# Expert routing weights by indirect DMA into device memory, inputs before outputs

## The reference

```python
s1 = jnp.einsum('thd,nd->thn', q[..., :PEER_HALF], subkeys1)
s2 = jnp.einsum('thd,nd->thn', q[..., PEER_HALF:], subkeys2)
v1, i1 = lax.top_k(s1, 16); v2, i2 = lax.top_k(s2, 16)
cand = v1[..., :, None] + v2[..., None, :]
vals, pos = lax.top_k(cand, 16)
ids = i1[pos // 16] * 128 + i2[pos % 16]
g = softmax(vals)
a = jnp.einsum('td,thkd->thk', xt, u_tab[ids])
hid = gelu(a) * g
y = jnp.einsum('thk,thkd->td', hid, v_tab[ids])
```

## Time and profile before

| | |
|---|---|
| median of three executions | 1153.8 us (1153.69 to 1155.7) |
| span of the profiled execution | 1152.6 us |
| instructions | 21629 |
| PE busy | 1102.2 us |
| DVE busy | 914.7 us |
| ACT busy | 479.6 us |
| POOL busy | 15.2 us |
| moved by DMA | 177.62 MB |

### The profile page before, as it was taken

One profiled execution on the slowest core, in us unless ns is written; L12 is line 12 of the kernel. 1 busy time (PEld: TensorE's weight loads), 2 busy tenths in 40 slices (PEclk: granted clock), 3 DMA queues, 4 the chain that ended last, 5 costly groups with the idle time before them and its releaser, 6 DMA issues.

```text
span 1152.6 us, 21629 instructions
## 1 busy us (share of the span) xinstructions
PE 1102.2 (96%) x7340; PEld 1004.3 (87%) x7340; DVE 914.7 (79%) x1706; ACT 479.6 (42%) x718; POOL 15.2 (1%) x20
## 2 busy tenths in 40 slices
PE   7779999799999999999998999999999999999996
PEld 7657898799999999999997888888888888888885
DVE  3246547668889998899898767777799999999997
ACT  4145444344445444434333444444344444444332
POOL 0310000000000000000000000000000000000000
PEclk9889999999999999999999999999999999999998
DMA  7664245432444434232223555555566656665563
GB/s 245 168 203 146 94 166 179 128 129 92 141 134 146 129 127 130 96 103 92 91 91 116 183 193 196 188 198 190 174 182 181 174 178 176 179 177 178 178 180 110
DMA packets 88102, 177.62 MB, mean 154 GB/s; under 512 B 16384, under 2 KB 44288, under 8 KB 88064
## 3 DMA queue, kind: packets, MB, share of 16 engines
q1 hardware_dynamic: 88064, 177.11, 48.1%
HBM read 176.03 MB, written 1.05 MB: 154 GB/s over the span
## 4 chain that ended last, share of the span: by engine, by line
PE 81%; DVE 7%; DMA 5%; SPq 2%; ACT 2%; issue 2%; DVEq 0%; ACTq 0%
PE ps L1328 29%; PE ps L1255 28%; PE ps L1222 12%; PE ps L1166 5%; PE ps L1307 4%; DMA w_raw<-in_w_in_dram 4%; SPq L260 1%; DVE w_lo L817 1%; DMA v_raw<-in_peer_v_dram 1%; DVE uT_raw L986 1%; PE ps L1120 1%; ACT w_hi L508 1%; PE ps L1159 1%; DVE v_lo L969 1%; ACT v_hi L602 1%
## 5 line engine op out<-in xcount | busy, mean ns | idle before, releaser
L1255 PE MATMUL ps<-act_hi,uT_hi 128*128 128x256 f32 x1024 | 295.3, 288 | 0.0
L1255 PE MATMUL ps<-act_hi,uT_lo 128*128 128x256 f32 x1024 | 289.8, 283 | 0.0
L1255 PE MATMUL ps<-act_lo,uT_hi 128*128 128x256 f32 x1024 | 289.6, 283 | 0.0
L1255 PEld LDWEIGHTS ps<-act_hi,uT_hi 128*128 128x128 f32 x1024 | 196.3, 192 | 2.1
L1255 PEld LDWEIGHTS ps<-act_lo,uT_hi 128*128 128x128 f32 x1024 | 196.2, 192 | 2.1
L1255 PEld LDWEIGHTS ps<-act_hi,uT_lo 128*128 128x128 f32 x1024 | 195.9, 191 | 0.0
L1328 PE MATMUL ps<-v_hi,hid_hi 128*128 128x512 f32 x512 | 164.8, 403 | 5.0 <-DVE v_lo L969 4.1
L1328 PE MATMUL ps<-v_hi,hid_lo 128*128 128x512 f32 x512 | 159.0, 392 | 0.0
L1328 PE MATMUL ps<-v_lo,hid_hi 128*128 128x512 f32 x512 | 158.7, 391 | 0.0
L817 DVE TENSOR_TENSOR w_lo<-w_raw,w_hi 128x2048 fp32r<-128x2048 f32 x34 | 77.9, 2291 | 86.9 <-ACT w_hi L508 86.9
L607 ACT ACTIVATE uT_hi<-uT_raw 128x1024 fp32r<-128x1024 f32 x53 | 56.3, 1062 | 184.4 <-DVE uT_raw L986 184.4
(11 more groups left out here) (165 smaller groups left out, 1642.5 us busy)
## 6 DMA issues: line engine op xcount, KB each, us to landing
v_raw<-in_peer_v_dram SPq DMA_DIRECT2D x92, 512.0 KB, 3.5
u_raw<-in_peer_u_dram SPq DMA_DIRECT2D x75, 512.0 KB, 3.3
u_raw<-in_peer_u_dram SPq DMA_DIRECT2D x212, 128.0 KB, 2.7
u_raw<-in_peer_v_dram SPq DMA_DIRECT2D x36, 512.0 KB, 3.2
w_raw<-in_w_in_dram SPq DMA_DIRECT2D x8, 2048.0 KB, 13.0
w_raw<-in_peer_wq_dram SPq DMA_DIRECT2D x4, 2048.0 KB, 9.1
w_raw<-in_w_out_dram SPq DMA_DIRECT2D x2, 2048.0 KB, 7.7
w_raw<-in_w_in_dram SPq DMA_DIRECT2D x2, 1024.0 KB, 7.2
```

Source lines behind the costliest of these rows:

```text
L1255: ins = pe.matmul(ps[:, bank, 0:T], (hi, hi, lo)[part][:, k, :], (act_hi, act_lo, act_hi)[part][:, k, :], start=(k == 0 and part == 0), st ...
```

## The change

The one-hot rows, their products, `G`, `early` and `settle` are gone. A table of 16,384 experts by 256 tokens in device memory (16.8 MB) takes their place.

- **Zeros.** SP writes zeros into it in 16 DMAs of 1 MB (`zero_part`): 8 behind the loads of the last 8 weight chunks, 8 behind the first loads of `u` in the pre stage.
- **Numbers.** The routing is done in two halves of four heads (`route`), and each ends with `cell`, the place of each picked expert and token in the table. The splits of `u` are spread over this by estimated costs.
- **Scatter.** POOL issues 256 indirect DMAs, one for each pick (8 heads of 16) and half of the tokens. Each adds 128 single weights from SBUF to 128 cells of the table. POOL waits for the half's `route_done`, and for head h until all scatters of the heads before have landed for these tokens.
- **Inputs.** The pre stage has 48 blocks (`NPRE`) with PE transposes. Then come 20 rounds (`ROUNDS`) of 4 blocks: one of them is transposed by PE, three by DVE. `H` keeps the gelu values of all 128 blocks.
- **Outputs.** 128 blocks one after another. For each one SP loads 128 KB of the table (`load_g`) and 512 KB of `v`; DVE multiplies the weights by `H` (`hidden`), rounds and subtracts. SP issues the first `load_g` only when all scatters have landed, and this wait stands ahead of the loads of `v` for blocks 1 to 3.

The core of the diff (memory addresses, the wiring of the loops and all deleted functions cut):

```diff
-NPRE = 42
-NDUR = 32
...
+NPRE = 48
+GROUP = 4
+ROUNDS = (NB - NPRE) // GROUP
+BODY = 4
...
+        def zero_part(n):
+
+            rows = NB * P // ZERO_DMAS
+            if n == 0:
+                sp.wait_ge(s["zero_set"], 2)
+            per = rows * T // P // ZEROS
+            part = table[n * rows:(n + 1) * rows, :].rearrange("(p r k) t -> p r (k t)", p=P, r=per)
+            sp.dma_start(part, zeros[:].unsqueeze(1).broadcast_to([P, per, ZEROS])).then_inc(s["zeroed"], 16)
...
+        for n in range(2, NPRE):
+
+            sp.wait_ge(s["u_read"], n - 1)
+            load_u(block_of(n), n % 2)
+            if n - 2 < ZERO_DMAS // 2:
+                zero_part(ZERO_DMAS // 2 + n - 2)
...
+        sp.wait_ge(s["u_read"], NPRE + ROUNDS)
+        load_v(0, 0)
+        for t in range(TB):
+            sp.wait_ge(s[f"scattered{t}"], 16 * SLOTS)
+        for b in range(2):
+            load_g(b, b)
+        for k in range(1, GROUP):
+            sp.wait_ge(s["u_turned"], (GROUP - 1) * (ROUNDS - 1) + k)
+            load_v(k, k)
+        with sp.Fori(0, NB // BODY - 1) as i:
+            for k in range(BODY):
+                sp.wait_ge(s["hid_done"], BODY * i + (k + 1))
+                load_g(BODY * i + (k + 2), k % 2)
+                sp.wait_ge(s["v_lo_done"], 2 * BODY * i + 2 * (k + 1))
+                load_v(BODY * i + (k + 4), k)
...
+        pool.wait_ge(s["zeroed"], 16 * ZERO_DMAS)
+        for h in range(PH):
+            if h % HALF_HEADS == 0:
+                pool.wait_ge(s["route_done"], h // HALF_HEADS + 1)
+            for t in range(TB):
+                if h:
+
+                    pool.wait_ge(s[f"scattered{t}"], 16 * TOPK * h)
+                for k in range(h * TOPK, (h + 1) * TOPK):
+                    pool.indirect_dma_start(
+                        out=table_cells, out_offset=bass.IndirectOffsetOnAxis(ap=cell[:, t, k:k + 1], axis=0),
+                        in_=gw[:, t, k:k + 1], in_offset=None, compute_op=ALU.add) \
+                        .then_inc(s[f"scattered{t}"], 16)
...
+            ch.step(dve.scalar_tensor_tensor(ids[:, :, ks], e1f[:, :, ks], float(NK), e2f[:, :, ks], ALU.mult, ALU.add))
+            ch.wait()
+            for t in range(TB):
+                ch.step(dve.tensor_scalar(cell[:, t, ks], ids[:, t, ks], float(T), column[:, t:t + 1],
+                                          ALU.mult, ALU.add))
...
+        with dve.Fori(0, ROUNDS) as i:
+            n = GROUP * i + NPRE
+            for k in range(1, GROUP):
+                before = 8 * NPRE if k == 1 else 0
+                turn(n + k, k, 16 * NQ * i + (before + 16 * NQ))
+                if k == 1:
+                    rest_uT(n, 6, 0)
+                else:
+                    rest_turned(n + (k - 1), k - 1)
+            rest_turned(n + (GROUP - 1), GROUP - 1)
...
+        def hidden(m, slot, landed, head):
+
+            cells = g_in[:, slot, :]
+            dve.wait_ge(s[f"g_in{slot}"], landed)
+            dve.tensor_tensor(cells, H[:, bass.ds(m * T, T)], cells, ALU.mult).then_inc(s["hid_m"], 1)
+            dve.wait_ge(s["hid_m"], m + 1)
+            if not head:
+
+                dve.wait_ge(s["y_done"], m - 1)
+            dve.tensor_copy(hid_hi[:, slot, :], cells).then_inc(s["hid_h"], 1)
+            dve.wait_ge(s["hid_h"], m + 1)
+            dve.tensor_tensor(hid_lo[:, slot, :], cells, hid_hi[:, slot, :].bitcast(F32),
+                              ALU.subtract).then_inc(s["hid_done"], 1)
...
+        def main_four(i, last):
+
+            for k in range(GROUP):
+                n = GROUP * i + (NPRE + k)
...
+                expert_inputs(k, 4 + k % 2)
+                if k == 1 and not last:
+                    transpose_u(16 * i + (8 * NPRE + 32), 0, 6)
...
+        with pe.Fori(0, (NB - 4) // 2) as i:
+            for k in range(2):
+                outputs_of(2 * i + (2 + k), k)
```

More of the change, by code:

```diff
@@ L301, in load_v, with load_g @@
             sp.dma_start(v_raw[:, slot, :], v_dram[bass.ds(b * P, P), :]).then_inc(s[f"v_in{slot}"], 16)
+        def load_g(b, slot):
+            sp.dma_start(g_in[:, slot, :], table[bass.ds(b * P, P), :]).then_inc(s[f"g_in{slot}"], 16)
         sp.wait_ge(s["mrg_lo_done"], 2)
[L305 to L366, removed]
@@ L541, in _ @@
                 copy_scores((hc - HC["w0"] - 3) // 2)
-        def pre_six(i, last):
-            for k in range(6):
-                if not (last and k == 5):
-                    round_uT(6 * i + k + 2, 6 - 4 * (k % 2), pre_slot(k + 2))
-                act.wait_ge(s["a_done"], 6 * i + k + 1)
-                act.activation(G[:, bass.ds((6 * i + (NB - NPRE + k)) * T, T)], ps[:, k % 2, 0:T],
-                               ACT.Gelu_apprx_tanh).then_inc(s["act_done"], 1)
-        with act.Fori(0, NPRE // 6 - 1) as i:
-            pre_six(i, False)
@@ new lines, in main_step, with round_v @@
+        def main_step(i, k, tail):
+            if k < 2:
+                round_turned((GROUP - 1) * i + (k + 2), k + 2)
+            elif not tail:
+                if k == 2:
+                    round_uT(i + (NPRE + 1), 6, uT_hi[:, 0])
+                else:
+                    round_turned((GROUP - 1) * i + GROUP, 1)
+            else:
+                round_v(k - 2, k - 2, 16)
+            gelu(GROUP * i + (NPRE + k), 4 + k % 2, GROUP * i + block_of(NPRE + k))
+        def round_v(slot, place, landed):
+            act.wait_ge(s[f"v_in{place}"], landed)
+            for d in range(2):
+                act.activation(v_hi[:, slot, d * 512:(d + 1) * 512], v_raw[:, place, d * 512:(d + 1) * 512],
+                               ACT.Copy).then_inc(s["v_hi_done"], 1)
@@ new lines, in _ @@
+        act.wait_ge(s["route_done"], 2)
+        with act.Fori(0, ROUNDS - 1) as i:
+            for k in range(GROUP):
+                main_step(i, k, False)
+        for k in range(GROUP):
+            main_step(ROUNDS - 1, k, True)
+        for m in range(2, BODY):
+            act.wait_ge(s["y_done"], m - 1)
+            round_v(m % 2, m, 16)
+        with act.Fori(1, NB // BODY) as i:
+            for k in range(BODY):
+                act.wait_ge(s["y_done"], BODY * i + (k - 1))
+                round_v(k % 2, k, 16 * i + 16)
@@ L973, in split_hidden @@
-        def split_hidden(n, slot, hidden, head):
-            if not head:
-                dve.wait_ge(s["y_done"], n - 1)
-            dve.tensor_copy(hid_hi[:, slot, :], hidden).then_inc(s["hid_h"], 1)
-            dve.wait_ge(s["hid_h"], n + 1)
-            dve.tensor_tensor(hid_lo[:, slot, :], hidden, hid_hi[:, slot, :].bitcast(F32),
-                              ALU.subtract).then_inc(s["hid_done"], 1)
-        def turn(landed, slot):
+        spent = 0.0
+        for hh in range(2):
+            for n in range(ROUTED[hh - 1] if hh else PICKED, ROUTED[hh]):
+                pick(n)
+                spent = pre_split(spent, PICK_COST[n % 3])
+            spent = route(hh, spent)
@@ L1284, in _ @@
-        ins.then_inc(s["routeT_done"], 1)
-        pe.wait_ge(s["uT_lo_done"], NPRE + 1)
-        transpose_u(8 * NPRE + 16, 1, 6)
-        expert_inputs(uT_hi[:, 0], uT_lo[:, 0], 4)
-        def during(part, i, slot, head):
-            h = PB * part + 2 * i + slot
-            n = NPRE + h
-            if not (head and slot == 0):
+                expert_inputs(k, k % 2)
+        pre_four(0, True, False)
+        with pe.Fori(1, NPRE // 4 - 1) as i:
+            pre_four(i, False, False)
+        pre_four(NPRE // 4 - 1, False, True)
```

499 lines of the change are left out of this document (179 added, 320 removed).

## The result

The new kernel takes 1201.3 us (median of four, 1198.2 to 1202.2) against 1154.0 us for the old one: 1.040 of its time (95% interval 1.0384 to 1.0414), so **4% slower**. The prediction was 1074 us, and faster. Its range, up to 1220 us, holds the result; its direction was wrong. The first rival happened.

A forecast was written before the change was run, and what follows sets the result against it. PE was taken to bound every stage after the projections, DVE close behind. Terms 276.8 + 181.4 + 5 + 2 + 248.4 + 348.2 + 10.6 gave a 1072.4 us span, 1073.6 us measured, if scatters finish in time; range 1062 to 1220.

The forecast's parts named there:

- The first rival: Scatters on POOL: too slow, whole kernel waits; time 712 + 256 r for r us a scatter, 1275 at 2.2; chance 0.26.
- the price of a scatter: POOL's time r for each of 256 scatters, taken as 1.3 us; at most 1.41 keeps the outputs on time.
- The bounds of 0.54 and 2.7: Ends for a scatter's us: DMA engines' need with a read and a write, and a small DMA's issue-to-landing time.
- The row of SP: Old trace: SP issues a DMA of 256 small pieces in 1.05 us, least 0.62; taken as nearest to a scatter.
- The lower bound: Scatter on the DMA engines: 128 cells at 34 ns a packet, 0.27 us, or 0.54 if adding reads and writes.
- The sign that the prediction gave for this rival: Between last input and first output: a hole in PE of 256 (r - 1.41) us, POOL busy to that point.
- The rest of the sum: Span with the table in time: 276.8 start, 181.4 pre, 5 zeros, 2 rounds' start, 248.4 rounds, 348.2 outputs, 10.6 tail.
- 181.4 + 5 + 2 + 248.4: Pre's 48 blocks at 3.78 us, zeros, start of the rounds, and 20 rounds at 12.42 us, all paced by PE.
- The zeros and the start of the rounds: Zero writes between loads of `u` in pre, 5 us (bounds 0 and 11); PE waiting for DVE after routing, 2 us.
- The third rival: Rounds: POOL and DVE get in each other's way; 1115 us, or POOL slowed as well; chance 0.10.
- the 41 us on DVE's side: Rounds: three DVE subtractions each wait up to 1.05 us for a scatter, 2.0 past the spare, over 20 rounds.
- The other direction: Rounds: POOL blocked by DVE for 3.7 of 12.42 us, turning a scatter's 1.3 us into 1.85.

The follow-up runs named there:

- the last one: The new kernel, still with adding scatters, with the rounds' three DVE subtractions reading their first input from PSUM instead of SBUF: 1191.7 us.

## Why the prediction was wrong

**The step that failed** is the price of a scatter: "Nearest is the issue of a DMA of many small pieces on SP: 256 pieces in 1.05 us, least 0.62. POOL has half as many pieces but must read an index for each; I take 1.3". It measured 1.54 us busy and 0.30 between two, 1.84, and 1.89 on the mean with the long ones. Above 1.41 the table is late; above 1.73 the kernel is slower. The bounds of 0.54 and 2.7 held, and 1.73 lay near their middle. Between such ends a guess decides the sign. An even spread over the bounds would have put (2.7 - 1.73) / (2.7 - 0.54) = 0.45 on the slower side, where the prediction had 0.26. Two things were missed. The row of SP times another way of issuing: the pieces cost little on POOL too (2.1 ns an index), but the instruction itself costs 1.27 us, by the estimate above. And the row's value was taken as the whole step, with nothing for the gap behind it. Of the 0.59 us that 1.3 fell short, 0.24 are busy time, 0.30 the gap and 0.05 the long scatters. Without the gap the step would be 1.59, below 1.73: the table late, but the kernel faster.

**The lower bound** was also argued from the wrong place. It priced the DMA engines, at 0.27 to 0.54 us a scatter. They did need about that: 8.5% of the span for 256 scatters is 102 us, 0.40 each. The engines were never the limit.

**The first rival** was right in mechanism and formula: 712 + 256 x 1.892 = 1196.4, against 1201.9 for the profiled execution. The 5.5 us between are the outputs (352.1 us from 837.15 to the end at 1189.3, for 348.2), the way from the last scatter to the first output (taken as 4 us behind it, measured 1.9 more), 0.2 in the tail and 0.6 outside the span, less 1.1 at the start. Of the outputs, 2.6 us are more than in the kernel with half of the scatters, which has no hole: the clock granted to PE was 0.52 in the hole and 0.66 in 837 to 845 us, and the first matmuls take up to 764 ns, where they take at most 467 there. The sign that the prediction gave for this rival was there too: a hole of 256 (1.89 - 1.41) = 123 us with POOL busy, measured 131.

**The rest of the sum** stands, as the kernel with half of the scatters shows: a span of 1064.0 for 1072.4.
- Pre and rounds: PE 427.3 us (276.3 to 703.6) for 181.4 + 5 + 2 + 248.4 = 436.8. The zeros and the start of the rounds cost nothing, which is 7 of the 9.5 us. The rest is mostly a slip in the sum: the transposes of three blocks, 3 x 0.90, lie before the first input (24 of the 544 matmuls of L1083) and were counted again in the 48 blocks. The blocks of the pre stage stay 3.78 apart behind the zeros, while the DMA engines were 91% busy at 341 GB/s (the new kernel's chain in order of time, then its stretch from 278 to 309 us):

```profile
278.64 2.87 PE ps L1172 x24
282.41 2.88 PE ps L1172 x24
```

```profile
278.00:309.00 31.00, 31.00 (x265) 31.00 (x264) 28.45 (x95) 13.36 (x19) 0.00 (x0) 1.00 0.91 341
```

- Outputs: 349.5 us for 348.2, tail 10.8 for 10.6. The multiplication and the 128 KB loads are covered, as argued from the earlier trace rows: in the new kernel DVE has about 0.4 us left before each copy, where it had 0.76. DVE's timeline of the new kernel:

```profile
901.70 0.42 DVE L939 TENSOR_TENSOR g_in<-H,g_in 128x256 f32<-128x256 f32 x1
902.48 0.29 DVE L944 CAST hid_hi<-g_in 128x256 fp32r<-128x256 f32 x1 [0.35 <-PE ps L1214]
...
905.27 0.29 DVE L944 CAST hid_hi<-g_in 128x256 fp32r<-128x256 f32 x1 [0.41 <-PE ps L1214]
```

- The first half of the routing was forecast to end at 348 us, and the first scatter came at 346.9.

**The third rival** was half right. POOL and DVE do meet at the subtraction with two inputs from SBUF, but it is POOL that waits. The subtractions keep their 1.2 us, and the rounds stay full on PE, so the 41 us on DVE's side did not come. The other direction was priced at 0.55 us a scatter and cost 8.3 / 255 = 0.03. The prediction drew the wrong end from the Trainium skill (SBUF — State Buffer, Who interferes with whom). That section says that a VectorE instruction with two SBUF inputs contends with a GpSimd instruction that reads SBUF. A scatter has its indices in SBUF, so it may be such an instruction: by the run with the input from PSUM the trace agrees, 0.96 us against 1.6 to 1.9, though no run shows which of POOL's reads waits. That the rounds would go undisturbed did not follow.

On the 1 us that the Trainium skill (DMA: Bandwidth & Descriptors, Latency and other measured facts) gives for the first byte of a GpSimd DMA, no row here shows a first byte, only how long POOL is busy with a scatter. Without adding that is 0.96 us; with adding it is 1.54, and POOL needs 0.30 more before the next. So 1 us was no price for a step.

What stays open: why adding costs 0.58 us on POOL. 144 packets in place of 32 explain 112 x 2.1 ns = 0.24 us, if a packet costs what an index does; the other 0.34 no run tells apart. Why DVE's subtractions hold an adding scatter up so much less is open too. Nor was a scatter with more than one weight for each partition tried, which would cut the number of instructions.

## What to carry to other kernels

Count the indirect DMAs of GpSimd and price them as instructions, 1.84 us each with adding and 1.26 without (half of the cells saved only 0.13); compare that sum with the stage that is to hide it before counting what the other engines save. Where it nearly fits, start the first one earlier and drop the adding where cells can't coincide: here that turned 4% slower into 4% faster. When the sign of a forecast hangs on one price for which no row exists, give both sides a chance by where the break-even lies between the bounds, not by the value that seems nearest.

## What the hardware showed unexpectedly

- An indirect DMA on POOL costs, with adding, 1.54 us for 128 indices and 1.40 for 64, so by estimate 1.27 us for itself and 2.1 ns an index. A gap of 0.30 us stands between two even when nothing else runs.
- VectorE lengthens a scatter by nearly the time of their overlap: from 0.96 to 1.89 us beside a subtraction from SBUF. A cast in SBUF does it too, by about half of the overlap (1.31 us beside 0.69), while the same subtraction from PSUM and DVE's transposes do not. With adding, the same subtractions cost a fourth of that: (202.06 / 125 - 199.41 / 130) x 125 / 58 = 0.18 us each, by POOL's busy time from 460 to 700 us in the new kernel and in the last one.
- Writing 8 MB of zeros between the loads of `u`, with the DMA engines 91% busy at 341 GB/s, cost PE nothing.
